# A two-block transformer layer in split fp32: turns one at a time between weight tiles, two modulation vectors summed by GpSimd

## What is computed

```python
mod   = silu(c) @ w_ada + b_ada            # w_ada is 2048 x 12288, 100 MB
mod_c = silu(c_ctx) @ w_ada + b_ada        # only its first two parts are used
sh_a, sc_a, gt_a, sh_f, sc_f, gt_f = split(mod, 6)
h  = rms_norm(x, g_attn) * (1 + sc_a) + sh_a
hc = rms_norm(ctx, g_attn) * (1 + csc_a) + csh_a
x  = x + gt_a * mixer(h, hc)               # 4 kinds of attention: na, gqa, mla, diff, 4 heads each
h  = rms_norm(x, g_ffn) * (1 + sc_f) + sh_f
x  = x + gt_f * ((silu(h @ wg) * (h @ wu)) @ wd)     # inner width 5632
x  = rms_norm(x, g_final)
# second block, of its own weights: two kinds of attention (moba, fox) of 8 heads each, gates,
# an output projection, a squared-relu feed-forward of inner width 8192, rms_norms
```

## Time and profile before

| | |
|---|---|
| runs | 3018.11, 3019.5, 3019.6 us, median 3019.5 |
| profiled execution | 3021.58 us, its span 3019.8 us |
| granted TensorE clock, mean | 0.977 of full speed |
| TensorE matmuls busy | 2844.6 us, 94% of the span |
| VectorE, ScalarE, GpSimd busy | 1649.6, 1155.2, 229.4 us |
| read from HBM | 573.43 MB |

### The profile page before, as it was taken

One profiled execution on the slowest core, in us unless ns is written; L12 is line 12 of the kernel. 1 busy time (PEld: TensorE's weight loads), 2 busy tenths in 40 slices (PEclk: granted clock), 3 DMA queues, 4 the chain that ended last, 5 costly groups with the idle time before them and its releaser, 6 DMA issues.

```text
span 3019.8 us, 34015 instructions
## 1 busy us (share of the span) xinstructions
PE 2844.6 (94%) x12864; PEld 2266.1 (75%) x12864; DVE 1649.6 (55%) x1929; ACT 1155.2 (38%) x1487; POOL 229.4 (8%) x239
## 2 busy tenths in 40 slices
PE   5899998989899999999989997999999999999997
PEld 2477777447778888888767886788787888888886
DVE  2348762456645555555574445554554665565565
ACT  2122232333434443444343443444444444444443
POOL 1125530010100000000060000000000000000000
PEclk9899999999999999999989999999999999999998
DMA  8759772766556555555536550455555565555552
GB/s 306 272 179 302 234 253 78 278 230 223 193 172 195 190 194 188 185 196 182 180 133 216 194 194 28 154 195 194 181 169 179 184 198 183 193 188 188 189 191 97
DMA packets 272282, 579.84 MB, mean 192 GB/s; under 512 B 9962, under 2 KB 12745, under 8 KB 265545
## 3 DMA queue, kind: packets, MB, share of 16 engines
q1 hardware_dynamic: 268272, 557.47, 55.7%
q0 software_dynamic: 3600, 21.19, 2.0%
q10 hardware_dynamic: 328, 0.09, 0.0%
HBM read 573.43 MB, written 5.28 MB: 192 GB/s over the span
## 4 chain that ended last, share of the span: by engine, by line
issue 63%; PE 25%; DVE 5%; DMA 2%; ACT 2%; DVEq 2%; POOL 1%; POOLq 0%; SPq 0%; ACTq 0%
PE bank L359 6%; PE bank L360 6%; PE bank L361 6%; DMA w_raw<-in_w_ada 1%; DVE proj_ctx L1471 1%; PE bank L644 1%; PE bank L1762 1%; PE bank L602 1%; DVE w_lo L355 1%; ACT probs L751 1%; PE bank L684 1%; PE bank L1771 0%; DVEq L792 0%; DVEq L1470 0%; PE bank L1784 0%
## 5 line engine op out<-in xcount | busy, mean ns | idle before, releaser
L355 DVE TENSOR_TENSOR w_lo<-w_raw,w_hi 128x1024 fp32r<-128x1024 f32 (+1 forms) x856 | 1043.1, 1238 | 717.1 <-ACT w_hi L347 705.4
L347 ACT ACTIVATE w_hi<-w_raw 128x1024 fp32r<-128x1024 f32 (+1 forms) x856 | 892.7, 1054 | 1245.7 <-PE bank L361 1164.2
L359 PE MATMUL bank<-w_hi,xa_hi 128*128 128x512 f32 (+1 forms) x2304 | 905.5, 393 | 18.7 <-DVE w_lo L355 14.0
L361 PE MATMUL bank<-w_hi,xa_lo 128*128 128x512 f32 (+1 forms) x2304 | 897.8, 390 | 0.0
L360 PE MATMUL bank<-w_lo,xa_hi 128*128 128x512 f32 (+1 forms) x2304 | 897.7, 390 | 0.0
L359 PEld LDWEIGHTS bank<-w_hi,xa_hi 128*128 128x128 f32 x2304 | 435.0, 189 | 127.8 <-issue 26.4
L361 PEld LDWEIGHTS bank<-w_hi,xa_lo 128*128 128x128 f32 x2304 | 434.6, 189 | 90.3
L360 PEld LDWEIGHTS bank<-w_lo,xa_hi 128*128 128x128 f32 x2304 | 435.0, 189 | 87.3
L359 PE MATMUL bank<-w_hi,ffn_act_hi 128*128 128x512 f32 x864 | 338.2, 391 | 7.9 <-DVE w_lo L355 7.9
L361 PE MATMUL bank<-w_hi,ffn_act_lo 128*128 128x512 f32 x864 | 337.6, 391 | 0.0
L360 PE MATMUL bank<-w_lo,ffn_act_hi 128*128 128x512 f32 x864 | 337.5, 391 | 0.0
(11 more groups left out here) (279 smaller groups left out, 1747.2 us busy)
## 6 DMA issues: line engine op xcount, KB each, us to landing
w_raw<-in_w_in SPq DMA_DIRECT2D x116, 1024.0 KB, 5.1
w_raw<-in_w_ada SPq DMA_DIRECT2D x96, 1024.0 KB, 5.3
w_raw<-in_w_up SPq DMA_DIRECT2D x64, 1024.0 KB, 5.2
w_raw<-in_w_down SPq DMA_DIRECT2D x64, 1024.0 KB, 5.1
w_raw<-in_ffn_wg SPq DMA_DIRECT2D x44, 1024.0 KB, 5.1
w_raw<-in_ffn_wu SPq DMA_DIRECT2D x44, 1024.0 KB, 5.1
w_raw<-in_ffn_wd SPq DMA_DIRECT2D x44, 1024.0 KB, 5.1
w_raw<-in_w_out SPq DMA_DIRECT2D x32, 1024.0 KB, 5.1
```

The source lines that it names most:

```text
L347: act.activation(whi[:, slot, ks, 0:w], raw[:, q, ks, 0:w], ACT.Copy)\
L355: dve.tensor_tensor(wlo[:, slot, ks, 0:w], raw[:, q, ks, 0:w], whi[:, slot, ks, 0:w].bitcast(F32), ALU.subtract).then_inc(sem("lo_made"), 1)
L359: pe.matmul(out, xh, wh, start=first, stop=False)
L361: return pe.matmul(out, xl, wh, start=False, stop=last)
```

## The change

1. **Bands first.** The na table's transpose, the 64 band matmuls and the na bias stand ahead of the first `w_ada` unit on TensorE, ScalarE and VectorE, and use bank 6.
2. **Turns spaced.** In the front each of the four turns stands alone behind a `w_ada` unit: turns 0 and 1 behind units 2 and 3 of the even chunk, turns 2 and 3 behind units 0 and 1 of the odd chunk. The early pieces stand behind units 2 and 3 of the odd chunk and 0 and 1 of the next even one. The loads of `w_in` move accordingly, and VectorE's list too.
3. **No strips.** `late_unit`, `late_take`, `bias_of` and `store_rows` go. The first attention uses banks 6 and 7 in turn, and its product of step d waits for the lo part of step d−2.
4. **Order in both attentions.** VectorE makes the lo part of the outputs behind the copy of `probs_T` and the normalisation instead of ahead of them; TensorE turns the diff outputs behind the products with v.
5. **`sc_f` by GpSimd, in the mixed stage.** Four chunks of 512 columns, each in eight steps with a 512 KB load on GpSimd's queue, one multiplication and two additions. Chunks 0 and 1 stand behind the last turn of the front, chunks 2 and 3 behind the normalisation of the mla rows. TensorE adds up at four fixed places of the unit list.
6. **`gt_f` by GpSimd, in the feed-forward.** Sixteen units of 1 MB on its own queue with two slots, each one multiplication and two or three additions. At the end of the feed-forward four matmuls with a matrix of ones sum and spread the vector, and VectorE adds the bias in four operations.
7. A number of semaphores are merged (`x_act`, `wf_split`, `fz_dve`, `fz_act`, `lam_dve`).

The core of the diff:

```diff
-        if c % 2 == 0 and c:
-            loads.append(("win", 0, c // 2 - 1))
+        if c >= 3 and c % 2:
+            loads.insert(-3, ("win", 0, c // 2 - 1))
...
+    for p, place in enumerate(((4, 2), (5, 3), (6, 3), (7, 3))):
+        at.append((next(i for i, n in enumerate(W) if MIX[n] == ("win",) + place), "pool", p))
...
@@ attn_pe, per step n @@
-                if A.wide() and n in LATE_AT:
-                    v, k = LATE_AT[n]
-                    if k == 0 and v:
-                        pe.wait_ge(sem("ada_rows"), N_ADA_1 + v)
-                    late_unit(pe, v, k)
-                    late_unit(pe, v, k + 1)
...
-                    wait(pe, T + "_out_lo", A.since(d))
-                    o = A.o_bank(d)
+                    wait(pe, T + "_out_lo", d - 1)
+                    o = ps[6 + d % 2]
...
@@ the front on TensorE @@
             for c in range(N_ADA_1):
+                g = c // 2 - 1
                 wait(pe, "ada_rows", c)
                 for q in range(4):
                     ada_unit(c, q)
-                    if c == 1:
-                        if q == 0:
-                            pe.wait_ge(sem("na_rpb_lo"), 1)
-                        for j in range(16 * q, 16 * q + 16):
-                            m = pe.matmul(ps[q][:, (j % 16) * 28:(j % 16) * 28 + 28], bandr[:, 63 - j:191 - j],
-                                          narpbr[:, :], start=True, stop=True)
-                        m.then_inc(sem("na_bands"), 1)
-                    if c >= 3 and c % 2:
-                        early_piece(pe, c // 2 - 1, q)
                     if q == 1 and c:
                         spread_row(c - 1)
-                    if q == 2 and c >= 2 and c % 2 == 0:
-                        turn_h_pe(pe, c // 2 - 1)
+                    if c >= 2 and c % 2 == 0:
+                        if q >= 2:
+                            turn_h_pe(pe, g, q - 2)
+                        elif c >= 4:
+                            early_piece(pe, g - 1, q + 2)
+                    elif c >= 3:
+                        if q < 2:
+                            turn_h_pe(pe, g, q + 2)
+                        else:
+                            early_piece(pe, g, q - 2)
+            early_piece(pe, 2, 2)
             spread_row(N_ADA_1 - 1)
+            early_piece(pe, 2, 3)
...
@@ win_copy on ScalarE and VectorE (na_q, na_k) @@
+                if col < 2 * NCH:
+                    act.wait_ge(sem("pool_summed"), N_LATE_P)
...
@@ GpSimd, mixed stage @@
+            def row_load(p, s):
+                col = 2 * D + (N_LATE_D + p) * NCH
+                b = (8 * p + s) % 3
+                pool.dma_start(pool_raw[b], w_ada_h[:, s, :, col:col + NCH]).then_inc(sem(f"pool_landed{b}"), 16)
+
+            def row_sum(p):
+                if p >= 2:
+                    pool.wait_ge(sem("ada_combined"), next(a for a in MAKER if MAKER[a] == ("pool", p - 2)) + 1)
+                for s in range(8):
+                    if s + 2 < 8:
+                        row_load(p, s + 2)
+                    b = (8 * p + s) % 3
+                    pool.wait_ge(sem(f"pool_landed{b}"), 16 * ((8 * p + s) // 3) + 16)
+                    w, acc = pool_raw[b], pool_acc[p % 2]
+                    pool.tensor_tensor(w, w, ccol[:, 2 * s:2 * s + 2].rearrange("p (k a) -> p k a", a=1)
+                                       .to_broadcast([P, 2, NCH]), ALU.mult)
+                    pool.drain()
+                    if s == 0:
+                        m = pool.tensor_tensor(acc, w[:, 0, :], w[:, 1, :], ALU.add)
+                    else:
+                        pool.tensor_tensor(acc, acc, w[:, 0, :], ALU.add)
+                        pool.drain()
+                        m = pool.tensor_tensor(acc, acc, w[:, 1, :], ALU.add)
+                    pool.drain()
+                m.then_inc(sem("pool_summed"), 1)
...
@@ GpSimd, first feed-forward @@
+            for u in range(16):
+                c, q = u // 4, u % 4
...
+                acc, w = gt_f[:, c * NCH:(c + 1) * NCH], gate_raw[u % 2]
+                pool.tensor_tensor(w[:, :, :], w[:, :, :], ccol[:, 4 * q:4 * q + 4].rearrange("p (k a) -> p k a", a=1)
+                                   .to_broadcast([P, KQ, NCH]), ALU.mult)
+                pool.drain()
+                pool.tensor_tensor(w[:, 0:2, :], w[:, 0:2, :], w[:, 2:4, :], ALU.add)
+                pool.drain()
+                if q == 0:
+                    pool.tensor_tensor(acc, w[:, 0, :], w[:, 1, :], ALU.add)
+                else:
+                    pool.tensor_tensor(acc, acc, w[:, 0, :], ALU.add)
+                    pool.drain()
+                    pool.tensor_tensor(acc, acc, w[:, 1, :], ALU.add)
+                pool.drain()
+                if u + 2 < 16:
+                    gate_load(u + 2)
...
@@ end of the first feed-forward, TensorE and VectorE @@
+                if q == 0:
+                    pe.wait_ge(sem("pool_summed"), N_LATE_P + 1)
+                    for c in range(4):
+                        m = pe.matmul(ps[c][:, :], ones[:, :].to_broadcast([P, P]), gt_f[:, c * NCH:(c + 1) * NCH],
+                                      start=True, stop=True)
+                    m.then_inc(sem("gate_spread"), 1)
...
+                if q == 0:
+                    dve.wait_ge(sem("gate_spread"), 1)
...
+                    for c in range(4):
+                        dve.tensor_tensor(gt_f[:, c4], ps[c][:, :], gate_b[:, c4], ALU.add)
```

More of the change, by code:

```diff
@@ L84 @@
 N_LOAD_1 = len(FRONT) // 4
+PER = [0, 0, 1, 1, 2, 0, 2, 0, 2, 0]
 def mixed_units():
-    per = [0, 0, 1, 1, 2, 0, 2, 0, 2, 0]
-    units, a = [], 4 * N_ADA_1
+    units, d = [], 0
     for c in range(1, len(WIN)):
@@ L93, in mixed_units @@
             units.append(("win", c, q))
-            for _ in range(per[c]):
-                units.append(("ada", a // 4, a % 4))
-                a += 1
-    assert a == 4 * N_ADA
+            for _ in range(PER[c]):
+                units.append(("ada", d // 4, d % 4))
+                d += 1
+    assert d == 4 * N_LATE_D
     return units
@@ L686, in attn_pe @@
                     m.then_inc(sem(T + "_out"), 1)
+                s = A.get(n - 4, lo_, hi_)
+                if s and s["d"] is not None and s["kind"] == "diff":
+                    pe.wait_ge(sem("diff_normed"), s["head"] + 1)
+                    for i in range(2):
+                        m = pe.transpose(ps[6 + s["d"] % 2][:, 256 + i * P:256 + i * P + P],
+                                         od[:, s["head"] % 2, i, :], ident[:, :])
+                    m.then_inc(sem("diff_turned"), 1)
                 q = n - hi_
@@ L1462, in multiply @@
                 dve.wait_ge(sem(f"landed{u % 4}"), 16 * (u // 4 + N_LOAD_1) + 16)
-                if k == 0 and c >= N_ADA_1 + 2:
-                    dve.wait_ge(sem("ada_combined"), c - 1)
+                if k == 0 and c >= 2:
+                    dve.wait_ge(sem("ada_combined"), next(a for a in MAKER if MAKER[a] == ("dve", c - 2)) + 1)
                 for j in range(KQ):
@@ L1984, in _ @@
             pool.drain().then_inc(sem("mla_normed"), 1)
+            for p in range(2, 4):
+                row_load(p, 0)
+                row_load(p, 1)
+                row_sum(p)
             for c, col in ((3, DF_Q), (4, DF_K)):
```

272 lines of the change are left out of this document (135 added, 137 removed).

## The result

The changed kernel takes 3089.9 us (median, 4 runs from 3081.54 to 3095.26), 1.0225 of the time before, 95% interval 1.0207 to 1.0244: 70 us slower, where +25 was forecast. Its profiled execution, the longest of the four, has a span of 3093.5 us, 73.7 longer than before.

A forecast was written before the change was run, and what follows sets the result against it. TensorE, busy for 94% of the span, was taken to bound the kernel. The terms −15, −28, −10, +53, +22, +3 gave +25 on the profiled 3021.6 us, 3046.6, said as 3044 for the median; range 2995 to 3088.

The forecast's parts named there:

- GpSimd beside VectorE: Mixed stage: GpSimd's sums delay VectorE's operations, a step taking 5.8 us and 16 steps 93 us: +53 us.
- full exclusion: Rival, mixed stage and feed-forward: GpSimd and VectorE durations add up, a step takes 7.1 us: +85, 3104 us, chance 0.12.
- DMA traffic: Mixed stage: 16.8 MB more of loads cost +12 us even where GpSimd hurts nobody, not added to the +53.
- Front: Front: spaced turns save 9 us and moved bands 6, together −15 us, bounds −5 and −20.
- The 6 us for the bands: Front: moving the 64 band matmuls, at most 12.8 us, to where TensorE waits lets about half come through, 6 us.
- First attention: First attention: without the strips the steps shorten, −28 us, bounds −18 and −33.
- the clock rival: Rival, first attention: without strips TensorE pauses and its clock falls, +15 to +20, about 3062 us, chance 0.07.
- Second attention: Second attention: VectorE's wait for ScalarE's hi part of the outputs is filled, −10 us, bounds −3 and −17.
- Feed-forward: Feed-forward: GpSimd's gate sum, 12.3 us a unit with four w_lo between, slows TensorE: +22 us, bounds 0 and +44.
- End of the feed-forward: End of the feed-forward: spreading matmuls and VectorE's additions ahead of the gate product, +3 us, bounds 0 and +5.
- the prediction's own case: Mixed stage and feed-forward: a step takes 5.8 us, a gate unit 12.3; +25, 3044 us, chance 0.52.
- The absorbed case: Rival, mixed stage and feed-forward: light exclusion, pauses absorbed, +28 and 0; kernel faster by 22, 2998 us, chance 0.22.

The follow-up runs named there:

- run 3: Changed kernel with all arithmetic of the sc_f sums on GpSimd but 6 loads in place of 32, three tiles used again and again: 3055.52 us, ratio 1.0104.
- run 2: Changed kernel with the 32 loads of the sc_f sums and the waits for them, but no arithmetic: 2996.77 us, ratio 0.9925.
- run 1: Changed kernel without the four sc_f sums in the mixed stage, neither loads nor arithmetic, result set to zero: 3001.65 us, ratio 0.9929.
- run 8: Kernel before with only the front changed: bands ahead of the first unit, turns spaced, loads of w_in moved: 3016.82 us, ratio 0.9986.
- run 9: Kernel before with turns spaced and loads of w_in moved, bands left behind the units of chunk 1: 3013.06 us, ratio 0.9976.
- run 4: Changed kernel with each sc_f load in one piece of 4 KB a partition in place of two of 2 KB, same bytes: 3079.34 us, ratio 1.0189.
- run 5: Changed kernel with each sc_f load in four pieces of 1 KB a partition: 3084.09 us, ratio 1.0204.
- run 6: Changed kernel whose gate sum in the feed-forward loads only its first two tiles and adds those again and again: 3098.11 us, ratio 1.0247.
- run 7: Kernel before with only VectorE's lo part of the outputs moved behind the probs_T copy and normalisation, both attentions: 3014.14 us, ratio 0.9969.
- run 11: Changed kernel with the sc_f sums and the gate sum given to VectorE, GpSimd only issuing 16 gate loads: 2997.32 us, ratio 0.9916.
- run 12: Changed kernel with the sc_f and gate sums given to VectorE and the bands back behind the units of chunk 1: 2994.76 us, ratio 0.9922.

## Why the prediction was wrong

The direction held, the value did not: +25 was said, +70 came, and the range ended at 3088. Against the trace (+73.7) the sum was 49 us short. The mixed stage alone accounts for 42, the front, the attentions and the end for another 20, and the feed-forward, forecast 12 too dear, hid part of that. Term by term:

- **GpSimd beside VectorE, mixed stage: +53 forecast, +94.6 in the trace. This is the step that failed.** It reads "a multiplication …, and two additions …: 4.36 us" as the whole of a step. The load that each of 24 steps issues on the same queue was left out: measured 0.74 us of issue, 0.55 ahead of it and about 2.0 us more idle time behind the next multiplication. The sums took not 93 us a pair but 139 (170.1 to 309.4 us), the second pair ended at 485, and TensorE, for which they stand at fixed places of its list, waited 43.8 us. The prediction had named this wait, but as a companion of full exclusion; it came without that. To this come 5 us at each change of chunk within a pair, for the landing of the first load. It is the step that put the time outside the range: without the loads (run 3) the kernel takes 3055.5 us, inside it. Where only the arithmetic runs (run 3), a step takes 5.8 us, as taken, and 16 steps 91.6 (93 said). Its price, 60 us above run 2, is near the 53 said, but partly by luck: 42 are waits, and 19 are TensorE's clock, for which the prediction had no term in this stage.
- **DMA traffic.** "+12 even where GpSimd hurts nobody" was wrong: run 2, with all 16.8 MB, has the stage 3.9 us longer than before and 5.2 shorter than run 1, which has none of them.
- **Front: −15 forecast, −4.7.** Its lower bound. The first unit starts at 37.6 us in place of 26.4, since TensorE waits 19.0 us for the tables of the bands. The turns are spaced as foreseen, and where a wait of 1.99 us stood between two turns there now is one for a tile. TensorE, from 66 us on, in the changed kernel:

```profile
67.29 0.66 PE L440 MATMUL bank<-identity,x_in 128*128 128x128 f32 x4
68.49 1.07 PE L1779 MATMUL bank<-w_raw,c_stationary 128*32 128x512 f32 x8 [0.55 <-DMA w_raw<-in_w_ada]
...
71.44 1.07 PE L1779 MATMUL bank<-w_raw,c_stationary 128*32 128x512 f32 x8 [1.20 <-DMA w_raw<-in_w_ada]
...
76.78 1.93 PE L1779 MATMUL bank<-w_raw,c_stationary 128*32 128x512 f32 x8 [3.69 <-DMA w_raw<-in_w_ada]
```

  The engine has exchanged one waiting for another: up to 170 us it waits 15.5 us for tiles of `w_ada`, and 7.4 for the `w_lo` of the early pieces (0.3 before). That the landing of tiles sets the end is read from these waits and those of runs 8 and 9; no run changed the landing. The 6 us for the bands were wrong: half was said to come through, none shows.
- **First attention: −28 forecast, −20.1,** and −26.4 and −26.3 in runs 1 and 2. The missing 6 us are clock: four steps of the changed kernel's profiled execution take 6.2 to 8.0 us, which are 5.2 to 5.3 in run 1, and fall into the window from 672 to 706 us with its clock of 0.60. The same steps in run 1:

```profile
590.00:620.00 30.00, 24.66 (x124) 15.54 (x124) 22.10 (x52) 13.79 (x47) 3.33 (x6) 0.98 0.00 1
```

  Before the fall TensorE had no strips and short pauses for the exponentials, in all these kernels alike; runs 4, 5 and 6 have the same code here as the changed kernel and gain 30.9, 26.9 and 26.5 us. So the clock rival came in part, once, and what decides whether it comes stays open. The greater loss of clock was in the mixed stage (20 us), where no rival had it.
- **Second attention: −10 forecast, −7.6,** by VectorE's order alone (run 7).
- **Feed-forward: +22 forecast, +9.7.** The unit was put at 12.3 us. Without its load it takes just that (run 6: 12.33), and the loss is 19.3. With the load it took 13.6, and yet cost less. The step that fails is one `w_lo` for each of GpSimd's operations, 4 a unit: with the pause behind the load it is 4.5, without 3.6. The same omission as in the mixed stage, with the sign turned: here nobody waits for GpSimd, so a pause is a gift.
- **End of the feed-forward:** +3 forecast, +1.9.

Of the rivals, full exclusion (3104) came nearest in time, for another reason. Where the arithmetic runs without loads, a step took 5.8 us and not 7.1 (run 3), a unit 12.3 and not 13.6 (run 6), both as the prediction's own case had them. The Trainium skill's rule ("SBUF — State Buffer", section "Who interferes with whom") is borne out in who holds up whom: VectorE's multiply-add beside GpSimd took 1.97 us for 0.75, its `w_lo` 2.52 for 1.23. That the one blocked waits for the whole of the other's operation is so at 805.27 in the kernel before, but over runs 3 and 6 the durations did not add up in full. The absorbed case can be dropped; of the lost clock 6 us came, in one stage of this execution.

Two rows had been read a little off, without weight for the sum. The seven multiply-adds at 288.10 do not run alone: the first two stand beside a GpSimd operation, and the five alone take 0.75 us each, one every 0.83, not 0.91, which makes the full sum of a step 6.9 us in place of 7.1. And of the two `w_lo` at 805.27 the first ended at 808.4, 1.1 us behind GpSimd's 807.3: it did its work behind GpSimd's operation, and not beside it.

That the pause comes from GpSimd writing out its own load was not shown; it is shown that it comes with the issue of a load, goes when the load goes, and hardly changes with the number of pieces of source, at the same number of packets. The Trainium skill, "DMA: Bandwidth & Descriptors", section "SWDGE vs HWDGE vs iDMA", says that for DMAs issued from GpSimd one of its cores computes the descriptors in software. No run here shows that, and none issued the same loads from another engine's queue.

## What to carry to other kernels

Cost a helper engine's step with everything on its queue, the loads it issues and the drain behind them too, then lay the sum of its steps beside the place where another engine waits for the result: here 24 steps with a load, 2.7 us dearer each, turned a loss of 64 into 95. Then add what TensorE's clock costs once it has to wait: 20 of the 95 us were the same matmuls at a lower clock. Whoever moves work to GpSimd should ask first whether the engine that it would hold up, here VectorE, has idle time between its own operations: 64 multiply-adds on VectorE, in the gaps of the feed-forward, cost 0.1 and 2.4 us (runs 11 and 12), while the same sum on GpSimd cost 5 to 14 us with its loads and 22 without. A wait that disappears in front of a stream of loads may come back as a wait for the stream, as in the front here.

## What was not expected of the hardware

- A load of 512 KB issued by GpSimd costs that engine 2.6 us where nothing contends (7.33 against 5.13 − 0.43 = 4.70 us) and 2.7 beside VectorE (8.5 against 5.8): its issue, 0.55 ahead of it, and idle time up to the operation behind the next drain (2.16 against 0.14 us, 24 and 8 steps). One, two or four pieces of source a partition, at 128 packets of 4096 bytes a load each time, give 2.34, 2.16 and 2.20 us.
- Taking GpSimd's loads away made a stage slower (19.3 us lost for 9.7, and for 3.2 to 11.8 in the other traces), because VectorE had used the pauses.
- GpSimd's sums cost TensorE not only waits: over the same 1352 matmuls its granted clock was 0.89 in place of 1.00, and they took 20.4 us longer.
